# DeltaNet scan on one core: the inverse's levels spread over four 64x64 quarters of TensorE, and X turned two heads at a time by full 128x128 transposes

## What is computed

```python
a_strict = jnp.where(strict, jnp.einsum('bhnid,bhnjd->bhnij', k, k) * decay * beta[..., :, None], 0.0)
rhs = jnp.concatenate([k * (beta * jnp.exp(gc))[..., None], v * beta[..., None]], axis=-1)
sol = lax.linalg.triangular_solve(a_strict, rhs, left_side=True, lower=True, unit_diagonal=True)
w, u = sol[..., :dk], sol[..., dk:]
...
def step(s, inp):
    v_new = u_n - jnp.einsum('bhcd,bhde->bhce', w_n, s)
    o_n = jnp.einsum('bhcd,bhde->bhce', qd_n, s) + jnp.einsum('bhij,bhje->bhie', attn_n, v_new)
    s = s * cd_n[..., None, None] + jnp.einsum('bhcd,bhce->bhde', kd_n, v_new)
```

## Time and profile before

| what | us |
|---|---|
| median of 3 runs | 4355.04 |
| lowest and highest | 4342.85, 4355.46 |
| the profiled execution | 4348.21 |
| its span, first to last instruction | 4346.2 |

### The profile page before, as it was taken

How to read it: one execution, slowest core, us unless ns; L and a number is a source line. 1 busy time by engine, 2 the same in 40 slices (tenths; PEclk the granted TensorE clock), 3 DMA queues, 4 the chain that set the end, 5 groups by cost and what they waited for, 6 DMA issues and landing times. The chain is left out here.

```text
span 4346.2 us, 102671 instructions
## 1 busy us (share of the span) xinstructions
PE 4004.5 (92%) x43885; PEld 3530.9 (81%) x43885; DVE 2292.1 (53%) x3978; ACT 1505.7 (35%) x2718; POOL 607.9 (14%) x755
## 2 busy tenths in 40 slices
PE   6999989999949998999998999989999869989998
PEld 5899977897828886899998999978887658867886
DVE  5655556354474434765556555564554464444434
ACT  4333343333253332433334333343332343333222
POOL 1221200232001100121211211100430011100000
PEclk8999999999969999999999999999999879999999
DMA  5433332000200002233223333321002000012332
GB/s 203 129 117 97 107 97 59 21 2 16 66 0 4 4 16 90 88 95 95 80 71 107 107 114 106 106 83 34 17 2 66 15 2 4 4 69 84 97 102 73
DMA packets 409068, 287.72 MB, mean 66 GB/s; under 512 B 13438, under 2 KB 366180, under 8 KB 408164
## 3 DMA queue, kind: packets, MB, share of 16 engines
q1 hardware_dynamic: 408676, 281.86, 21.3%
HBM read 270.27 MB, written 11.53 MB: 65 GB/s over the span
## 5 line engine op out<-in xcount | busy, mean ns | idle before, releaser
L793 ACT ACTIVATE w_hi<-w_raw 128x512 fp32r<-128x512 f32 (+1 forms) x724 | 405.0, 612 | 647.1 <-POOL w_raw L777 347.3
L800 DVE TENSOR_TENSOR w_lo<-w_raw,w_hi 128x512 fp32r<-128x512 f32 (+1 forms) x724 | 481.9, 705 | 174.5 <-ACT w_hi L793 174.5
L908 PE MATMUL PS<-x_hi,w_hi 128*128 128x384 f32 x1680 | 562.2, 335 | 0.0
L908 PE MATMUL PS<-x_lo,w_hi 128*128 128x384 f32 x1680 | 561.3, 334 | 0.0
L908 PE MATMUL PS<-x_hi,w_lo 128*128 128x384 f32 x1680 | 561.2, 334 | 0.0
L1174 DVE SCALAR_TENSOR_TENSOR arena<-PS,mod,arena 128x256 f32<-128x256 f32 (+1 forms) x336 | 198.2, 631 | 340.1 <-PE PS L921 339.9
L1089 DVE TENSOR_TENSOR hid_flat<-hid_flat,PS 128x384 f32<-128x384 f32 (+1 forms) x454 | 245.9, 556 | 245.6 <-PE PS L908 154.0
L921 PE MATMUL PS<-hidden_hi,w_hi 128*128 128x256 f32 (+1 forms) x1232 | 342.0, 347 | 7.6 <-DVE hidden_lo L1141 5.7
L921 PE MATMUL PS<-hidden_hi,w_lo 128*128 128x256 f32 (+1 forms) x1232 | 337.0, 343 | 0.0
L921 PE MATMUL PS<-hidden_lo,w_hi 128*128 128x256 f32 (+1 forms) x1232 | 336.9, 343 | 0.0
L908 PEld LDWEIGHTS PS<-x_lo,w_hi 128*128 128x128 f32 x1680 | 315.4, 188 | 0.2
(11 more groups left out here) (356 smaller groups left out, 8218.0 us busy)
## 6 DMA issues: line engine op xcount, KB each, us to landing
w_raw<-in_ffn_w_dram SPq DMA_DIRECT2D x512, 256.0 KB, 4.0
arena<-in_ada_w_dram SPq DMA_DIRECT2D x120, 512.0 KB, 5.7
arena<-in_w_in_dram SPq DMA_DIRECT2D x64, 512.0 KB, 4.0
arena<-in_ada_w_dram SPq DMA_DIRECT2D x6, 2048.0 KB, 14.5
arena<-in_w_out_dram SPq DMA_DIRECT2D x16, 512.0 KB, 3.8
h_save<-arena SPq DMA_DIRECT2D x16, 384.0 KB, 2.3
arena<-h_save SPq DMA_DIRECT2D x2, 3072.0 KB, 15.3
w_raw<-in_ffn_w_dram SPq DMA_DIRECT2D x32, 128.0 KB, 2.3
```

Of the source, the lines that this page charges most:

```text
L793: nc.scalar.activation(w_hi[:, high_place(n, what, j), 0:size], w_raw[:, load_of[what] % 2, place, 0:size], ACT.Copy).then_inc(w_high_read ...
L800: nc.vector.tensor_tensor(w_lo[:, b, place, 0:size], w_raw[:, b, place, 0:size], w_hi[:, high_place(n, what, j), 0:size].bitcast(F32), ALU ...
L908: mm = pe.matmul(PS[:, 4 * b + bank, 0:half], w[wo], x_split[xo][:, j, k, 0:half], start=(k == 0 and q == 0), stop=(k == KH - 1 and q == 2))
```

## The change

The change rewrites the five levels. X is turned by two full 128x128 transposes for each direction, each over a pair of heads, against the full identity. A full transpose moves the columns of head e of a pair to partition half e, and the block that stood in half p to column block p; so the turned X and `TP` now hold the heads in another arrangement. The products of a level go from rows `p` to rows `e` (and back), over all four quarters, and the two row halves write to different banks: `two_banks` spreads the four small results of a direction over two banks, 256 columns apart. Lower times X now writes banks c and c+1, X times lower banks c+2 and c+3, and the turn goes to bank c+2 where it went to bank c. After level 5 the turn is still made of products with `id_c`.

```diff
+        HEADS_DN = [(w, e, p) for w in range(2) for e in range(2) for p in range(2)]
+
+        def two_banks(b, w):
+            return PS[:, b:b + 2, :].rearrange("p a c -> p (a c)").rearrange("p (u c) -> p u c", u=DN_H)[:, :, 0:w]
...
-                    for l in range(n):
-                        if l > 0:
-                            for g in range(2):
-                                c = 4 * g
-                                pe.wait_ge(x_ready[g], xs + l)
-                                for u in range(DN_H):
-                                    for p in HALVES:
-                                        mm = pe.matmul(packed(PS[p, c + 1, 0:128], l)[:, u], AT[g][p, u, p],
-                                                       even(XP[g][p, u, :], l, "p"), start=True, stop=True)
-                                mm.then_inc(tx_summed[g], 1)
...
+                        if l < n - 1:
+                            for w in range(2):
+                                pair = XP[g][:, 2 * w:2 * w + 2, :].rearrange("p u t -> p (u t)")
+                                mm = pe.transpose(PS[:, 4 * g + 2, w * P:(w + 1) * P], pair, ident[:, :])
...
+                        for w, e, p in HEADS_DN:
+                            u, rows = 2 * w + e, HALVES[p]
+                            mm = pe.matmul(level_blocks(4 * g, l)[HALVES[e], 2 * p + w], AT[g][rows, u, rows],
+                                           even(XP[g][rows, u, :], l, "p"), start=True, stop=True)
...
+                        for w, p, e in HEADS_DN:
+                            rows = HALVES[e]
+                            mm = pe.matmul(two_banks(4 * g + 2, 32)[HALVES[p], 2 * e + w], YP[g][rows, 2 * w + p, :],
+                                           TP[g][rows, 2 * p + w, :], start=True, stop=True)
...
+                    for l in range(1, n):
                         for g in range(2):
...
+                            turn_x(g, l - 1)
+                            lower_times_x(g, l)
+                        for g in range(2):
+                            x_times_lower(g, l)
+                    for g in range(2):
+                        turn_x(g, n - 1)
...
-                            x = even(XP[g], l)
-                            v.tensor_tensor(x, x, packed(PS[:, 4 * g + 2, 0:128], l), ALU.subtract).then_inc(x_ready[g], 1)
...
+                            for e in range(2):
+                                x = XP[g].rearrange("p (w e) (b s j) -> p e w b s j", e=2, s=2, j=1 << l)[:, e, :, :, 0, :]
+                                ins = v.tensor_tensor(x, x, level_blocks(4 * g + 2, l)[:, 2 * e:2 * e + 2], ALU.subtract)
+                            ins.then_inc(x_ready[g], 1)
```

More of the change, by code:

```diff
@@ L1596, in even @@
             return v[:, :, :, 0, :] if axes == "p u" else v[:, :, 0, :]
-        def packed(t, l):
-            return t.rearrange("p (u b j) -> p u b j", u=4, j=1 << l)
         def blocks(b, p=slice(0, P)):
@@ L1716, in pool_dn, with level_blocks @@
                     step(first, a, w, i, True)
-        def pe_dn(pe, layer):
-            def times(b, width, lhs, rhs):
-                for u in range(DN_H):
-                    for p in HALVES:
-                        mm = pe.matmul(PS[p, b, u * width:(u + 1) * width], lhs(u, p), rhs(u, p), start=True, stop=True)
-                return mm
+        HEADS_DN = [(w, e, p) for w in range(2) for e in range(2) for p in range(2)]
+        def two_banks(b, w):
+            return PS[:, b:b + 2, :].rearrange("p a c -> p (a c)").rearrange("p (u c) -> p u c", u=DN_H)[:, :, 0:w]
+        def level_blocks(b, l):
+            return two_banks(b, 32).rearrange("p u (b j) -> p u b j", j=1 << l)
+        def pe_dn(pe, layer):
             def spread_gates(it):
@@ new lines, in turn_x @@
+                    def turn_x(g, l):
+                        pe.wait_ge(x_ready[g], xs + l + 1)
+                        if l == 0:
+                            pe.wait_ge(attn_ready[g], it + 1)
+                            pe.wait_ge(kst_ready[g], own + 1)
+                        if l < n - 1:
+                            for w in range(2):
+                                pair = XP[g][:, 2 * w:2 * w + 2, :].rearrange("p u t -> p (u t)")
+                                mm = pe.transpose(PS[:, 4 * g + 2, w * P:(w + 1) * P], pair, ident[:, :])
+                        else:
+                            for u in range(DN_H):
+                                for p in HALVES:
+                                    mm = pe.matmul(blocks(4 * g + 2, p)[:, u], XP[g][p, u, :], id_c[p], start=True, stop=True)
+                        mm.then_inc(x_turned[g], 1)
@@ new lines, in lower_times_x @@
+                    def lower_times_x(g, l):
+                        pe.wait_ge(x_ready[g], xs + l)
+                        if l == 1:
+                            pe.wait_ge(at_moved[g], it + 1)
+                        for w, e, p in HEADS_DN:
+                            u, rows = 2 * w + e, HALVES[p]
+                            mm = pe.matmul(level_blocks(4 * g, l)[HALVES[e], 2 * p + w], AT[g][rows, u, rows],
+                                           even(XP[g][rows, u, :], l, "p"), start=True, stop=True)
+                        mm.then_inc(tx_summed[g], 1)
@@ L1909, in step @@
                         v.tensor_tensor(ATTN[g], DMT[g], bank(4 * g + 2), ALU.mult).then_inc(attn_ready[g], 1)
+                        u = slice(g * DN_H, (g + 1) * DN_H)
+                        row = lambda t: bc(t[:, bass.ds(first + i, 1), u].rearrange("p o u -> p (o u)"), 2, [P, DN_H, P])
+                        dve.wait_ge(ks_ready[g], it + 1)
+                        v.tensor_tensor(AV[g], bank(4 * g + 3), row(begc), ALU.mult).then_inc(kst_ready[g], 1)
                     for l in range(1, n):
```

30 lines of the change are left out of this document (7 added, 23 removed).

## The result

The changed kernel takes 4360.5 us (median of 11 runs, 4345.81 to 4388.13), the kernel before 4346.78 beside it (11 runs, 4338.15 to 4355.46): 1.0042 times as long, 95% interval 1.0023 to 1.0061, a small loss that is clear of the noise. The forecast was 30 us faster, and 0.05 stood on slower.

A forecast was written before the change was run, and what follows sets the result against it. TensorE's blocks and the chain through them bound each level; 2.80 and 3.16 us gained a step, less entry and exit, left 2.30 and 2.75, six steps each: 30.3 us. Forecast 4321 us, range 4306 to 4340.

The forecast's parts named there:

- The level: One of the five levels after the change: 2.33 us, gaining 0.70 in layer 0 and 0.79 in layer 1.
- two transposes to the next block: Turn of one direction in a level: two full transposes take 0.39 us until the next block.
- 16 records of four quarters: One direction's product block in a level: issued in 0.24 us, last record started at 0.21, ended at 0.43.
- the subtraction pair: VectorE's split subtraction in a level: two 64-column instructions take 0.36 us, against 0.29 as one.
- the switch into transposes: TensorE going from quarters to full transposes in a level: 0.15 us from the last record's start.
- rival 2: Seams in the levels cost what the bounds allow: subtraction pairs not overlapped, full drain each switch; 4338 us, chance 0.09.
- a pair at its upper bound: Split subtraction in a level as two full instructions: 0.58 us instead of 0.36.
- rival 3: Four quarters do not overlap in blocks of 16 records; level 3.06 us, 4358 to 4361 us, chance 0.05.
- The entry: AV moved ahead of a step's first turn; level 2's turn 0.43 us late in layer 0, 0.34 in layer 1.
- The exit: Behind the last turn of a step, the distance of the two subtractions makes direction 1's part 0.07 us late.
- Rival 4: Fewer records and more gaps in levels drop TensorE's clock to 0.50 over the whole phase; 4439 us, chance 0.05.

The follow-up runs named there:

- late_av: Changed kernel with the first turn waiting for ATTN alone and each direction's AV computed just before its level-1 mask; 4300.19 us, 0.9909 of the kernel before.
- levels_only: Changed kernel plus four unread constant products of 224 columns in each level, none at the entry; 4407.27 us, 1.0164 of the kernel before.
- before_av_moved: Kernel before with only AV moved ahead of the levels and the first turn waiting for it; 4382.33 us, 1.0094 of the kernel before.
- entry_only: Changed kernel plus eight unread constant products of 128 columns ahead of a step's first turn, none elsewhere; 4321.96 us, 0.9957 of the kernel before.
- fill: Changed kernel plus eight unread constant products behind a step's first turn and eight in each level; 4328.44 us, 0.9964 of the kernel before.
- lean_fill: Changed kernel plus four unread constant products of 224 columns in each level and four behind a step's first turn; 4316.5 us, 0.9942 of the kernel before.
- turn_products: Changed kernel with X turned by eight four-quarter products a direction instead of two full transposes; 4375.53 us, 1.0063 of the kernel before.
- products_lean: Changed kernel with turns by four-quarter products and constant products of 224 columns at entry and in levels; 4350.54 us, 1.0028 of the kernel before.

## Why the prediction was wrong, and what of it was right

**The level.** Forecast 2.33, measured 2.31. Its parts: two transposes to the next block 0.39, measured 0.37 (960.95 to 961.32); 16 records of four quarters issued in 0.24, measured 0.25 (962.05 to 962.30); the subtraction pair 0.36, measured 0.35; the switch into transposes 0.15 behind the last start, measured 0.36 from block to turn (962.90 to 963.26), which is the forecast's 0.21 and 0.15. The drain of rival 2, a pair at its upper bound, and rival 3 (quarters that do not overlap) are refuted by the same rows. Levels 2 to 5 together gave 2.92 (958.63 to 967.82, the last turn, against 12.11), for a forecast of 2.80; the last of them is shorter, since the turn after it needs no switch.

**The entry and the exit.** Turn 0 was to be 0.72 late against L1735 (834.52 for 833.8); it is 2.17 behind it instead of 1.38, so 0.79. The turn of level 2 was to lose 0.43 and loses 0.50 (4.92 against 4.42 behind L1735). The exit was to lose 0.07 and loses 0.15 (967.82 to 969.80 is 1.98, before 1.83). 2.92 - 0.50 - 0.15 = 2.27 a step, forecast 2.30; in layer 1 2.65, forecast 2.75. Twelve steps at 1.00 make 29.5, forecast 30.3.

**The step that failed** is the forecast's section on the entry, where the change costs. It worked out when the first turns would come, and priced the delay at 0.43 us a step. It did not go on to say what TensorE does meanwhile: 0.34 of waiting becomes 1.14, and another 0.42 follows behind one short block. What that costs is the clock: 64 us in the profiled execution, twice the 29.5 us that the change gives at 1.00.

**Rival 4** had the right mechanism and the wrong place. It looked for the cause in the levels, with 29 records a us instead of 32, and found the RWKV-7 stretch at 1.00 with such levels. That comparison was sound as far as it went: with short waits at the entry such levels stand at 1.00 over 392 us (late_av). The rival was priced as a fall over the whole phase, 10 us a step by the 128x128 products alone. It came as a fall in eight of twelve steps, and in the step shown it took more from the levels (5.0) than from the products, of which it covers 16. It was given 0.05 because only one source of it was looked at; the range, which left it out, missed for the same reason. A partial fall, some steps of twelve, had no price at all: at about 8 us for each fall (64.2 over eight), five of them put the forecast's 4318 near the 4360 of the median run. By the mean clock of each run (0.941 to 0.954) the number of falls differs from run to run: 11 runs of this kernel spread over 42 us, those of the kernel before over 17.

**Open.** Which steps fall, with equal waits at each entry, is not settled, nor is why `levels_only`, which is the changed kernel with work added, was slower than it. (Its profiled execution, 4380.54 us at a mean clock of 0.945, is the fastest of its four; the others ran at 0.934 to 0.938.) Why a fall lasts longer in levels on four quarters is open too. That the falls start from the waits is shown both ways: made in the old kernel (before_av_moved), and, but for one fall in 36 steps, gone in the new one when either wait is filled; gone as well when the first is halved and the second removed (late_av).

## What to carry to other kernels

An edit that moves a hidden instruction ahead of TensorE's first block has two prices: the delay, and the wait that TensorE then makes, which can drop its clock for many times the wait's own length. Before pricing such a fall by the work that follows, look at every place where the edit lengthens TensorE's idle time, and read from the stretches where a fall begins. First take the instruction out of the wait again, as `late_av` does by moving it behind the first turns; constants in the wait are the second choice here (4316.5 and 4321.96 against 4300.19).

## What the runs showed of the hardware that was not expected

- Two waits of TensorE of 1.14 and 0.39 to 0.53 us were followed by stretches at the granted clock 0.50 (1.2 instead of 2.4 GHz) in 6 to 10 of the 12 steps of five kernels. Most lasted 10.2 to 27.3 us, three 3.4 or 6.8. With only one of the two waits there was one fall in 36 steps (entry_only, fill, lean_fill).
- Six more falls, of 3.4 to 13.7 us, began within or at most 1.3 us behind single idle times of 1.2 to 2.1 us in the middle of levels (turn_products, products_lean). Most such gaps were followed by none: products_lean has 38 of over 0.5 us and one fall.
- During such a stretch TensorE was busy in 20.50 of 20.50 us, and the clock stayed at 0.50 all the same. How long it stayed went with the levels' form: 6.8 to 10.2 us with products on two quarters (before_av_moved, six falls), 17.1 to 27.3 with four quarters and transposes (changed kernel, eight falls), and 20.5 in six of the eight falls at the entry with four quarters and no transposes (turn_products).
- At 0.50 a level of four quarters takes 3.47 us for 2.31, 1.5 times, and the old one 5.12 for 3.02, 1.7 times; 16 products of 128x128 take 3.68 for 2.05, 1.8 times.
- TensorE stood still for up to 2.09 us (turn_products) and 1.57 us (products_lean) inside a level with no semaphore to wait for (issue), where the turn of a direction had 16 records instead of two.
